# Half of the first modulation as one-column matmuls on TensorE in a hybrid decoder block

## The chip, the core and the metric

The kernel runs on one NeuronCore of a Trainium2 chip. The metric is the device time of one launch in microseconds, as the median of several runs. TensorE (PE) multiplies, VectorE (DVE) and ScalarE (ACT) work elementwise, GpSimd (POOL) works elementwise and issues a few transfers, and SyncE (SP) issues nearly all transfers.

## What is computed

```python
mod = jax.nn.silu(c) @ w_ada[l] + b_ada[l]
sh1, sc1, ga1, sh2, sc2, ga2 = jnp.split(mod[:, None, :], 6, axis=-1)
h = rmsnorm(x, ln_mix_g[l]) * (1.0 + sc1) + sh1
(rq, rk, rv, rg, nq_, nkc, nvc, ...) = jnp.split(h @ w_in[l], IN_SPLITS, axis=-1)
...
k_cmp = compress(kc, pe_k, w1_k, w2_k)
...
x = x + ga1 * (jnp.concatenate([y_ret, y_nsa], axis=-1) @ w_out[l])
h2 = rmsnorm(x, ln_ffn_g[l]) * (1.0 + sc2) + sh2
x = x + ga2 * ((jax.nn.silu(h2 @ w_ff_gate[l]) * (h2 @ w_ff_up[l])) @ w_ff_down[l])
return rmsnorm(x, ln_final_g)
```

There are 512 tokens of width 1024 and one row `c` of 1024 values. `w_ada` is 1024 x 6144; its six column blocks of 1024 give the six modulation vectors. All is float32. This case is about `sc1` (the scale half) and `sh1` (the shift half), which are needed before the first projection can start.

## The kernel before, in words

Every large product is made of three matmuls (`product`, L1085): each operand is split into a high and a low part, and high x high, high x low and low x high are added in PSUM. A unit of weights comes by one transfer of 512 KB into one of seven slots of `raw`, ACT writes its high part to `wh` (`high`, L420), and POOL writes the rest to `wl` (`low`, L370). For the activations `hTh` and `hTl` play the same parts, and they are feature-major: eight blocks `k` of 128 features by 512 tokens.

The front end of the kernel makes `hTh` and `hTl`. The tokens are normalised, PE transposes them (L1120) block by block, and ACT copies them to `xT` (L454). Then the modulation is applied in four steps `q`, each for two blocks `k = 2q` and `2q + 1`:

- **The weights.** SP loads sixteen pieces of `w_ada` of 512 KB into the eight slots of `early` (`load_early`, L313). Piece `j = 4q + 2kh + i` holds the rows of contraction half `kh` for 256 columns of step `q`; `i = 0` is the scale half, `i = 1` the shift half. A slot is loaded again when DVE has used it (`ada_used`).
- **The sums over the contraction.** `ada_early` (L682) on DVE multiplies a 128x256 part of a piece by a column of `cs` (silu of `c`) and adds it to `acc`: 16 operations for each step, 8 of the scale half and 8 of the shift half, taken in turn. They are spread over the step before by hand: the constant `AHEAD` and the ranges at L751 to L766 say how many stand before `mod_columns`, and between and behind the two `h_low`.
- **The sum over the partitions.** `modulation(q)` (L1103) on PE does it with four fp32 matmuls of one column, `acc` as the stationary operand and a column of ones as the moving one (`sum_columns`, L1097).
- **Applying it.** DVE adds the bias (`mod_columns`, L712, L716 and L720) into `mods`; ACT scales and shifts block `k` into `hf` (L462) and copies it to `hTh` (L465); DVE subtracts for `hTl` (`h_low`, L746, L748). Between two blocks ACT does the high part of the next unit of weights, whose low part POOL makes.

On PE `modulation(q + 1)` stands in the first projection chunk: the loop over units `v` at L1155 has, for `v` = 0, 1, 2, the products of tokens tile 0 and 1, then `modulation(v + 1)`, then those of tiles 2 and 3. `modulation(0)` stands among the transposes, before those of block 6. So each step is a ring: `mods` of step `q`, `hf`, `hTh`, `hTl`, the products of tiles 0 and 1 with block `2q + 1`, `modulation(q + 1)`, `mods` of step `q + 1`.

```python
                for t in range(TT):
                    if v < UPC - 1 and t == TT // 2:
                        modulation(q + 1)
```

After the fourth step DVE goes on with the other modulation vectors (`ada`, L696), whose weights share the ring `raw` with the units, so that each free slot waits for DVE or for POOL (`refill`, L295). ACT takes the first chunk out of PSUM, does the high parts of units 7 and 8, and then issues eight transfers of 256-byte rows (`load_blocks`, L501) that gather the blocks for the compression. What follows on ACT, and through it on PE, stands behind these issues.

## Time and profile before

| what | value |
|---|---|
| runs of the kernel | 825.2, 827.97, 830.14 us; median 827.97 |
| span of the profiled execution | 822.2 us |
| PE busy | 726.4 us (88%) |
| DVE busy | 323.9 us (39%) |
| ACT busy | 259.1 us (32%) |
| POOL busy | 266.8 us (32%) |

The own time of the profiled execution was not recorded beside its span; the runs lie 3.0 to 7.9 us above the span. The busy shares are means over the whole kernel: in the first 60 us, and around 93 to 147 us, PE has long stretches without work, and in most of the rest it has none.

### The profile page before, as it was taken

To read this page: it belongs to the slowest core of one execution; us is meant where nothing else is said; L and a number is where in the kernel's file an instruction comes from. 1 tells how busy PE (TensorE), PEld (TensorE's weight loads), DVE (VectorE), ACT (ScalarE), POOL (GpSimd) and SP (SyncE) were. 2 spreads that over 40 slices of the span, in tenths; PEclk is the share of its full clock that TensorE was granted. 3 is DMA by queue.
4 is the path that set the end of the run, shared out by engine and by line. 5 is a ranking of instruction groups with operands and counts; after the bars stand their busy time and mean duration, and the time that the engine had idled before them with its cause. 6 is when DMAs were issued, how large, how long until landed. Compare 5 with 4: busy or idle time off the path is not lost.

```text
span 822.2 us, 9608 instructions
## 1 busy us (share of the span) xinstructions
PE 726.4 (88%) x3715; PEld 600.0 (73%) x3715; DVE 323.9 (39%) x529; ACT 259.1 (32%) x515; POOL 266.8 (32%) x126
## 2 busy tenths in 40 slices
PE   2789400888999999999999999999999999999995
PEld 2567300678877777878888988888888888888884
DVE  4769300887653335755235301100000003943215
ACT  4433000332335335464244432222222222333222
POOL 3327000522005000211072254444444443755531
PEclk9979855899999999999999999999999999999998
DMA  9948600556633000000643052333233331332002
GB/s 317 361 171 259 233 18 18 184 186 211 215 113 103 1 2 26 1 1 2 205 119 87 2 146 86 101 103 98 86 99 102 103 103 52 128 103 94 9 1 102
DMA packets 78372, 89.39 MB, mean 109 GB/s; under 512 B 7072, under 2 KB 62072, under 8 KB 78200
## 3 DMA queue, kind: packets, MB, share of 16 engines
q1 hardware_dynamic: 73040, 86.10, 32.4%
q10 hardware_dynamic: 4872, 1.61, 0.8%
q0 software_dynamic: 416, 1.08, 0.3%
q8 instruction: 29, 0.48, 0.3%
q14 instruction: 15, 0.12, 0.1%
HBM read 86.16 MB, written 2.62 MB: 108 GB/s over the span
## 4 chain that ended last, share of the span: by engine, by line
PE 61%; DVE 1%; ACT 1%; issue 1%; POOL 0%; POOLq 0%; DVEq 0%
PE ps L1413 10%; PE ps L1414 10%; PE ps L1412 10%; PE ps L1087 8%; PE ps L1089 7%; PE ps L1088 7%; PE ps L1246 3%; PE ps L1234 2%; PE ps L1279 1%; PE ps L1269 1%; PE ps L1224 1%; ACT xb L667 0%; PE ps L1391 0%; POOL rstd L381 0%; PE ps L1289 0%
## 5 line engine op out<-in xcount | busy, mean ns | idle before, releaser
L376 POOL TENSOR_TENSOR wl<-raw,wh 128x1024 fp32r<-128x1024 f32 (+1 forms) x94 | 238.2, 2540 | 389.4 <-ACT wh L430 389.2
L430 ACT ACTIVATE wh<-raw 128x1024 fp32r<-128x1024 f32 (+1 forms) x94 | 97.1, 1037 | 192.2 <-PE ps L1414 74.0
L1087 PE MATMUL ps<-wh,hTh 128*128 128x512 f32 (+1 forms) x224 | 93.8, 419 | 65.3 <-ACT stage L483 54.2
L1412 PE MATMUL ps<-hTh,wh 128*128 128x512 f32 (+1 forms) x384 | 142.8, 372 | 0.0
L1413 PE MATMUL ps<-hTl,wh 128*128 128x512 f32 (+1 forms) x384 | 142.6, 371 | 0.0
L1414 PE MATMUL ps<-hTh,wl 128*128 128x512 f32 (+1 forms) x384 | 142.6, 371 | 0.0
L1087 PEld LDWEIGHTS ps<-wh,hTh 128*128 128x128 f32 x224 | 45.0, 201 | 76.9 <-issue 60.8
L1052 DVE TENSOR_TENSOR act<-ps,sg 128x512 f32<-128x512 f32 x22 | 15.2, 692 | 212.3 <-PE ps L1414 212.3
L1088 PE MATMUL ps<-wl,hTh 128*128 128x512 f32 (+1 forms) x224 | 88.6, 395 | 0.0
L1089 PE MATMUL ps<-wh,hTl 128*128 128x512 f32 (+1 forms) x224 | 88.5, 395 | 0.0
L1412 PEld LDWEIGHTS ps<-hTh,wh 128*128 128x128 f32 x384 | 72.3, 188 | 12.6
L1413 PEld LDWEIGHTS ps<-hTl,wh 128*128 128x128 f32 x384 | 72.3, 188 | 12.4
L1414 PEld LDWEIGHTS ps<-hTh,wl 128*128 128x128 f32 x384 | 72.3, 188 | 12.4
L1087 PE MATMUL ps<-wh,ah 128*128 128x512 f32 x176 | 68.5, 389 | 0.0
L1088 PE MATMUL ps<-wl,ah 128*128 128x512 f32 x176 | 68.5, 389 | 0.0
L1089 PE MATMUL ps<-wh,al 128*128 128x512 f32 x176 | 68.5, 389 | 0.0
L566 ACT ACTIVATE PT<-ps 128x128 f32<-128x128 f32 (+3 forms) x64 | 28.1, 439 | 89.9 <-PE ps L1234 89.7
L875 DVE TENSOR_REDUCE mn<-ps 128x1 f32<-128x128 f32 (+3 forms) x64 | 31.3, 489 | 60.3 <-PE ps L1224 57.6
L1089 PEld LDWEIGHTS ps<-wh,hTl 128*128 128x128 f32 x224 | 44.9, 200 | 8.8
L1088 PEld LDWEIGHTS ps<-wl,hTh 128*128 128x128 f32 x224 | 45.1, 201 | 6.7 <-issue 0.2
L710 DVE SCALAR_TENSOR_TENSOR acc<-raw,cs,acc 128x1024 f32<-128x1024 f32 x28 | 47.1, 1682 | 3.3 <-DMA raw<-in_w_ada 2.0
L777 DVE TENSOR_TENSOR raw<-raw,ga 128x1024 f32<-128x1024 f32 x30 | 48.2, 1632 | 0.0
(185 smaller groups left out, 975.0 us busy)
## 6 DMA issues: line engine op xcount, KB each, us to landing
raw<-in_w_ada SPq DMA_DIRECT2D x32, 512.0 KB, 5.6
raw<-in_w_ff_gate SPq DMA_DIRECT2D x22, 512.0 KB, 3.8
raw<-in_w_ff_up SPq DMA_DIRECT2D x22, 512.0 KB, 3.7
raw<-in_w_ff_down SPq DMA_DIRECT2D x22, 512.0 KB, 3.3
raw<-in_w_in SPq DMA_DIRECT2D x20, 512.0 KB, 5.7
early<-in_w_ada SPq DMA_DIRECT2D x16, 512.0 KB, 9.7
raw<-in_w_out SPq DMA_DIRECT2D x8, 512.0 KB, 3.3
xs<-in_x SPq DMA_DIRECT2D x4, 512.0 KB, 6.0
```

The source lines that it names most:

```text
L376: pool.tensor_tensor(lo, raw[:, slot, 0:n], hi.bitcast(F32), ALU.subtract).then_inc(w_lo, 1)
L430: a.activation(split(u, n)[0], raw[:, slot, 0:n], ACT.Copy).then_inc(w_hi, 1)
L566: a.activation(PT[:, n % 2, 0:w], ps[:, 2, 0:w], ACT.Copy).then_inc(pT_ok, 1)
L710: d.scalar_tensor_tensor(dst, raw[:, slot, :], cs[:, k:k + 1], dst, ALU.mult, ALU.add).then_inc(ada_used, 1)
L777: d.tensor_tensor(raw[:, slot, :], raw[:, slot, :], ga[:, :], ALU.mult).then_inc(w_scaled, 1)
L875: d.tensor_reduce(mn[:, n % 8:n % 8 + 1], ps[:, s_bank(n), 0:w], AX.X, ALU.min).then_inc(s_min, 1)
L1087: mm(o, ah_, bh_, start=first, stop=False)
L1088: mm(o, ah_, bl_, start=False, stop=False)
L1089: return mm(o, al_, bh_, start=False, stop=last)
L1412: mm(o, hi[:, ks], hTh[:, k, c0:c1], start=k == 0, stop=False)
L1413: mm(o, hi[:, ks], hTl[:, k, c0:c1], start=False, stop=False)
L1414: ins = mm(o, lo[:, ks], hTh[:, k, c0:c1], start=False, stop=k == KT - 1)
```

## The change

In each step the shift half no longer goes through `acc`. PE takes the loaded pieces of `early` as the stationary operand, 128x128 at a time, and a column of `cs` as the moving one, and adds the eight parts of the contraction in PSUM: 16 one-column fp32 matmuls in each step. The scale half stays on DVE, 8 operations in each step in place of 16, and PE sums it with two of the four former matmuls. The slots of the shift half are now free when PE has done its matmuls (`shift_sum`), and `AHEAD` and the ranges are halved.

```diff
-AHEAD = 4
+AHEAD = 2
-ADA_OPS = 4 * ADA_START
+ADA_OPS = 2 * ADA_START
...
-        return 8 * (j // 2 + 1) - (j + 1) % 2 if j < ADA_START else ADA_OPS + j - ADA_START + 1
+        return 4 * (j // 2 + 1) if j < ADA_START else ADA_OPS + j - ADA_START + 1
...
-                if j >= EARLY:
+                q, kh, i = j // 4, j // 2 % 2, j % 2
+                if j >= EARLY and i == 0:
                     sp.wait_ge(ada_used, ada_ops(j - EARLY))
-                q, kh, i = j // 4, j // 2 % 2, j % 2
+                elif j >= EARLY:
+                    sp.wait_ge(shift_sum, q - 1)
...
-                for o in ops:
-                    p, (kk, i) = 2 * q + o // 8, divmod(o % 8, 2)
-                    j, k = 2 * p + i, 4 * (p % 2) + kk
+                for k in ops:
+                    kh, kk = divmod(k, 4)
+                    j = 4 * q + 2 * kh
...
-                    dst = acc[:, i, 2 * q * P:2 * (q + 1) * P]
+                    dst = acc[:, 0, 2 * q * P:2 * (q + 1) * P]
...
-                        d.wait_ge(ada_used, 16 * q + o - 1)
+                        d.wait_ge(ada_used, 8 * q + k)
...
-            ada_early(0, range(16))
+            ada_early(0, range(KT))
...
-                    ada_early(q + 1, range(AHEAD, AHEAD + 3))
+                    ada_early(q + 1, range(AHEAD, AHEAD + 2))
                 h_low(2 * q)
                 if q < UPC - 1:
-                    ada_early(q + 1, range(AHEAD + 3, AHEAD + 5))
+                    ada_early(q + 1, range(AHEAD + 2, AHEAD + 3))
                 h_low(2 * q + 1)
                 if q < UPC - 1:
-                    ada_early(q + 1, range(AHEAD + 5, 16))
+                    ada_early(q + 1, range(AHEAD + 3, KT))
...
-                pe.wait_ge(ada_used, 16 * (q + 1))
                 if q:
                     pe.wait_ge(mod_read, q)
-                sum_columns(0, 4 * q, (2 * q, 2 * q + 1))
-                sum_columns(1, 4 * q + 2, (2 * q, 2 * q + 1)).then_inc(mod_sum, 1)
+                else:
+                    pe.wait_ge(c_silu, 1)
+                for b in range(2):
+                    for k in range(KT):
+                        kh, kk = divmod(k, 4)
+                        j = 4 * q + 2 * kh + 1
+                        if b == 0 and kk == 0:
+                            pe.wait_ge(early_in[j % EARLY], 16 * (j // EARLY + 1))
+                        c0 = (2 * kk + b) * P
+                        ins = mm(ps[:, 7, 4 * q + 2 + b:4 * q + 3 + b], early[:, j % EARLY, c0:c0 + P], cs[:, k:k + 1],
+                                 start=k == 0, stop=k == KT - 1)
+                ins.then_inc(shift_sum, 1)
+                pe.wait_ge(ada_used, 8 * (q + 1))
+                sum_columns(0, 4 * q, (2 * q, 2 * q + 1)).then_inc(mod_sum, 1)
```

The order on PE around `modulation(0)`: L1120 are the transposes, L1100 the one-column matmuls of `modulation`, and the 128x512 rows are the products of unit 0. Before:

```order
L1120 MATMUL ps<-cst,xs 128x128 x24
L1100 MATMUL ps<-ones,acc 128x1 x4
L1120 MATMUL ps<-cst,xs 128x128 x8
L1087 MATMUL ps<-wh,hTh 128x512
L1088 MATMUL ps<-wl,hTh 128x512
```

And in the changed kernel, where the lines have moved down by 3 to 14:

```order
L1134 MATMUL ps<-cst,xs 128x128 x24
L1119 MATMUL ps<-cs,early 128x1 x16
L1103 MATMUL ps<-ones,acc 128x1 x2
L1134 MATMUL ps<-cst,xs 128x128 x8
L1090 MATMUL ps<-wh,hTh 128x512
L1091 MATMUL ps<-wl,hTh 128x512
```

The four one-column matmuls have become eighteen at the same place; at the three later places, behind 12, 36 and 60 matmuls of the projection, the same happens. The order on DVE in the first step (L716 and L720 make `mods`, L748 is `h_low`), before:

```order
L691 TENSOR_SCALAR acc<-early,cs 128x256 x2
L694 SCALAR_TENSOR_TENSOR acc<-early,cs,acc 128x256 x2
L716 TENSOR_TENSOR mods<-ps,cols 128x2
L720 TENSOR_TENSOR mods<-mods,cols 128x2
L716 TENSOR_TENSOR mods<-ps,cols 128x2
L694 SCALAR_TENSOR_TENSOR acc<-early,cs,acc 128x256 x3
L748 TENSOR_TENSOR hTl<-hf,hTh 128x512
L694 SCALAR_TENSOR_TENSOR acc<-early,cs,acc 128x256 x2
L748 TENSOR_TENSOR hTl<-hf,hTh 128x512
L694 SCALAR_TENSOR_TENSOR acc<-early,cs,acc 128x256 x7
```

And in the changed kernel:

```order
L694 TENSOR_SCALAR acc<-early,cs 128x256
L697 SCALAR_TENSOR_TENSOR acc<-early,cs,acc 128x256
L719 TENSOR_TENSOR mods<-ps,cols 128x2
L723 TENSOR_TENSOR mods<-mods,cols 128x2
L719 TENSOR_TENSOR mods<-ps,cols 128x2
L697 SCALAR_TENSOR_TENSOR acc<-early,cs,acc 128x256 x2
L751 TENSOR_TENSOR hTl<-hf,hTh 128x512
L697 SCALAR_TENSOR_TENSOR acc<-early,cs,acc 128x256
L751 TENSOR_TENSOR hTl<-hf,hTh 128x512
L697 SCALAR_TENSOR_TENSOR acc<-early,cs,acc 128x256 x3
```

The places stay, and the counts go from 4, 3, 2, 7 to 2, 2, 1, 3. On SP the order of the transfers stays, and the third group of pieces now waits for two engines in turn (in the kernel before, all four wait for `ada_used`):

```order
L308 DMA raw<-in_w_in 128x2x512
L322 DMA early<-in_w_ada 128x4x256 [waits ada_used]
L322 DMA early<-in_w_ada 128x4x256 [waits shift_sum]
L322 DMA early<-in_w_ada 128x4x256 [waits ada_used]
L322 DMA early<-in_w_ada 128x4x256 [waits shift_sum]
L335 DMA cst<-in_consts 128x902
L308 DMA raw<-in_w_in 128x2x512
```

Behind the waiting pieces stand, in the queue, the constants, the units of weights 2 and 3, and the first loads of `ada`.

## Rows read from the trace of the kernel before

**Rows 1.** The page: span and part 1 (busy us, share, instructions).

```profile
span 822.2 us, 9608 instructions
PE 726.4 (88%) x3715; PEld 600.0 (73%) x3715; DVE 323.9 (39%) x529; ACT 259.1 (32%) x515; POOL 266.8 (32%) x126
```

**Rows 2.** Waits, 0 to 70 us: us in total, times, longest.

```profile
ACT hf L462 <- DVE mods L716: 21.9, 3, 8.2
DVE mods L716 <- PE ps L1100: 3.6, 3, 1.7
```

**Rows 3.** Timeline of ACT: start, us, instruction, idle before it and releaser.

```profile
24.90 0.60 ACT L454 ACTIVATE xT<-ps 128x512 f32<-128x512 f32 x1 [0.25 <-PE ps L1120]
25.40 0.80 ACT L462 ACTIVATE hf<-xT,mods 128x512 f32<-128x512 f32 x1
...
36.45 0.82 ACT L462 ACTIVATE hf<-xT,mods 128x512 f32<-128x512 f32 x1 [7.28 <-DVE mods L716]
...
48.46 0.81 ACT L462 ACTIVATE hf<-xT,mods 128x512 f32<-128x512 f32 x1 [8.21 <-DVE mods L716]
...
58.63 0.82 ACT L462 ACTIVATE hf<-xT,mods 128x512 f32<-128x512 f32 x1 [6.38 <-DVE mods L716]
```

**Rows 4.** Timeline of PE: the four modulations and what stands ahead of them.

```profile
21.35 1.71 PE L1100 MATMUL ps<-ones,acc 128*128 128x1 f32 x8
...
31.20 0.79 PE L1087 MATMUL ps<-wh,hTh 128*128 128x512 f32 x1 [1.85 <-DVE hTl L748]
...
35.01 0.94 PE L1100 MATMUL ps<-ones,acc 128*128 128x1 f32 x8
...
42.26 0.79 PE L1087 MATMUL ps<-wh,hTh 128*128 128x512 f32 x1 [2.53 <-DVE hTl L748]
...
46.26 1.70 PE L1100 MATMUL ps<-ones,acc 128*128 128x1 f32 x8
...
54.30 0.49 PE L1087 MATMUL ps<-wh,hTh 128*128 128x512 f32 x1 [0.93 <-DVE hTl L748]
...
57.08 1.05 PE L1100 MATMUL ps<-ones,acc 128*128 128x1 f32 x8 [0.42 <-DVE acc L694]
```

**Rows 5.** Timeline of DVE: early sums, `h_low`, and the first operation of `ada`.

```profile
15.38 5.62 DVE L694 SCALAR_TENSOR_TENSOR acc<-early,cs,acc 128x256 f32<-128x256 f32 x14
...
40.28 1.92 DVE L748 TENSOR_TENSOR hTl<-hf,hTh 128x512 fp32r<-128x512 f32 x1 [0.84 <-ACT hTh L465]
42.13 2.85 DVE L694 SCALAR_TENSOR_TENSOR acc<-early,cs,acc 128x256 f32<-128x256 f32 x7
...
61.51 0.69 DVE L748 TENSOR_TENSOR hTl<-hf,hTh 128x512 fp32r<-128x512 f32 x1 [0.68 <-ACT hTh L465]
62.12 0.75 DVE L707 TENSOR_SCALAR acc<-raw,cs 128x1024 f32<-128x1024 f32 x1
```

**Rows 6.** Windows: us, busy time by engine, granted clock, DMA share, GB/s.

```profile
41.00:42.00 1.00, 0.00 (x0) 0.00 (x0) 1.00 (x1) 0.00 (x0) 1.00 (x2) 0.79 1.04 408
42.00:51.00 9.00, 8.74 (x25) 7.20 (x26) 6.90 (x21) 2.51 (x4) 1.40 (x1) 0.50 0.76 292
51.00:52.00 1.00, 1.00 (x4) 0.81 (x3) 0.45 (x2) 0.97 (x2) 0.97 (x1) 0.59 0.00 0
```

**Rows 7.** Timeline of PE: long series of small fp32 matmuls, later in the kernel.

```profile
192.72 7.25 PE L1191 MATMUL ps<-flatT,w 128*128 128x64 f32 x64
...
223.11 1.84 PE L1100 MATMUL ps<-ones,acc 128*128 128x1 f32 x16
```

**Rows 8.** Timeline of ACT from 78 to 144 us: `load_blocks`.

```profile
77.96 1.06 ACT L430 ACTIVATE wh<-raw 128x1024 fp32r<-128x1024 f32 x1 [4.88 <-DMA raw<-in_w_in]
...
78.80 22.50 ACTq L512 DMA_DIRECT2D flat<-kv_scratch  x1
101.33 6.97 ACTq L511 DMA_DIRECT2D flat<-kv_scratch  x1
```

**Rows 9.** Timeline of SP: pieces 12 to 15 of `early`.

```profile
27.20 7.28 SPq L319 DMA_DIRECT2D early<-in_w_ada  x4
```

More of the change, by code:

```diff
@@ L251, in block_kernel @@
         y_ps, y_scaled = sem("y_ps"), sem("y_scaled")
+        shift_sum = sem("shift_sum")
         dve_step = sem("dve_step")
```

## The prediction

> **What bounds the kernel now.** I read the page first. PE is busy for 88% of the span and DVE for 39% [rows 1], which says nothing yet about a change that moves work from DVE to PE: what counts is who is waited for in the first 60 us. So I read the waits of 0 to 70 us. The largest on ACT is for `mods`, 21.9 us in three waits, and DVE itself makes `mods` only after waiting for the one-column matmuls L1100 on PE [rows 2]. Then I followed the ring of one step through the timelines of ACT, DVE and PE. The first blocks of the four steps start on ACT at 25.40, 36.45, 48.46 and 58.63 us [rows 3]. In the step that begins at 36.45, the second `h_low` ends at 40.28 + 1.92 = 42.20 us and releases PE at 42.26; PE does nine matmuls of 512 columns until 46.26, then the modulation for 1.70 us, and ACT starts the next step at 48.46 [rows 3 to 5]. DVE had finished its seven sums at 42.13 + 2.85 = 44.98 us, 1.3 us before PE came to the modulation [rows 4, 5]. So in this ring PE is on the path and the early sums of DVE are not. Only in the last step does PE wait for DVE, for 0.42 us [rows 4]. For `modulation(0)` both are level: the fourteen sums and what precedes them end at 15.38 + 5.62 = 21.0, the transposes at 21.35 [rows 4, 5].
>
> The end of this ring is passed on in full. The first `ada` operation starts on DVE as the last `h_low` ends, at 62.1 us [rows 5]. The slot of unit 8 comes free through that chain of `ada` operations, ACT waits 4.88 us for unit 8, and right behind it stand the gather transfers, whose issuing holds ACT for 66 us, eight of them at 7 us or more each [rows 8]. Nothing in that stretch can catch up a late start.
>
> **TensorE's clock.** One modulation of four matmuls (eight records) takes 1.70 to 1.71 us at 21.35 and 46.26, and 0.94 to 1.05 us at 35.01 and 57.08 [rows 4]. The window of 42 to 51 us shows a granted clock of 0.50, which is the 1.2 GHz level [rows 6]; the row at 21.35 costs the same, so PE is slow there too (the record shows 1.00 up to 41 us, where it has no event yet). The nine matmuls ahead of a modulation take 35.01 - 31.20 = 3.81 and 46.26 - 42.26 = 4.00 us, slow, and 57.08 - 0.42 - 54.30 = 2.36 us, fast. So one fp32 matmul of one column costs 1.71 / 4 = 0.43 us slow and 0.94 / 4 = 0.235 us fast. In a longer fast series eight of them take 1.84 us, 0.23 each, and 32 fp32 matmuls of 64 columns take 7.25 us, also 0.23 each [rows 7]: the price is that of loading the stationary operand, and does not fall with the number of columns.
>
> **The change, part by part.**
>
> *Removed:* two of the four `sum_columns` matmuls and eight sums on DVE in each step. A sum costs 5.62 / 14 = 0.40 us [rows 5], so DVE gets back 8 x 0.40 = 3.2 us in each step, 12.8 in all. Only the 0.42 us for which PE waited counts; the rest lay beside PE. The new wait in each sum, for the sum just before it rather than for the last but one, may make each up to 0.1 us dearer; eight of them are still shorter than sixteen were. If PE were no longer in front, this cover would be gone, but it gets longer.
>
> *Added:* sixteen one-column matmuls in each step. No row shows one with `early` as the stationary operand, but L1100 has the same form, fp32, 128x128 against 128x1. I take its price. Eighteen then cost 18 x 0.43 = 7.7 us slow or 18 x 0.235 = 4.2 us fast. They stand in PE's queue ahead of `mods`, and behind them ACT's `hf`, DVE's `h_low` and PE's own products.
>
> *Step 0.* The shift pieces 1 and 3 have long landed, as DVE already sums from pieces 0 to 3 from 15.38 us without a wait. PE is slow at 21.35: 7.7 - 1.7 = **+6.0** (fast: +2.5). The transposes of blocks 6 and 7 are behind it, and ACT must copy block 7 before the first `hf`, as it does at 24.90 [rows 3], so the whole is passed on.
>
> *Step 1.* Before, nine matmuls slow (3.81) and then a fast modulation of 0.94. The clock rose just ahead of it. In the changed kernel PE comes out of 7.7 us of small matmuls and transposes, which had not raised the clock at 21.35 either, has a gap as before, and does only nine dense matmuls. I take slow: 7.7 - 0.9 = **+6.8** (fast: 4.2 - 0.9 = +3.3).
>
> *Step 2.* Before, all slow: 4.00 + 1.70 = 5.70. Behind the long modulation PE has fifteen slow products (6.4 us at 0.43) with hardly a gap before the second `h_low` comes, 5.8 us after `mods` (36.4 to 42.2); such a run raised the clock before. I take the nine fast (2.4) and, as the columns leave the array nearly empty, a clock that falls within them: three quarters fast, 18 x 0.284 = 5.1. That is 7.5 - 5.7 = **+1.8** (all fast: 6.6 - 5.7 = +0.9; all slow: 3.9 + 7.7 - 5.7 = +5.9).
>
> *Step 3.* Before, fast: 2.36 + 0.42 + 1.05 = 3.83. Now 7.5: **+3.7** (all fast: 6.6 - 3.8 = +2.8; all slow: 11.6 - 3.8 = +7.8).
>
> *Transfers.* Piece 9 now waits for PE's sixteen of step 0, to about 21.35 + 16 x 0.43 = 28 us, and piece 13 for those of step 1, to about 48 us; the four pieces 12 to 15 had been issued from 27.20 to 34.5 us before [rows 9]. Queued behind piece 13 are two more pieces, unit 3, unit 4, unit 5 and three `ada` loads: with it nine loads of 0.5 MB, 4.7 MB, which at the 408 GB/s of [rows 6] take 12 us, to 60. The first of them to be needed is unit 3, by ACT early in step 2 at about 65 us by the sum above. I cost it at nothing; if that cover were gone, it would be a few us more.
>
> **The sum:** 6.0 + 6.8 + 1.8 + 3.7 = +18.3 us. Against the profiled span it is 822.2 + 18.3 = 840.5; the runs lie 3 to 8 us above the span, the median 5.8, so 828.0 + 18.3 = **846 us**. The bounds are 2.5 + 3.3 + 0.9 + 2.8 = +9.5 (fast throughout, 837.5) and 6.0 + 6.8 + 5.9 + 7.8 = +26.5 (slow throughout, 854.5).
>
> **The rivals.**
>
> *A. The columns are nearly free (not slower).* One mechanism: the stationary operand is loaded beside the matmul before, and a matmul of one column then costs next to nothing. The modulations would shrink from 1.7 + 0.9 + 1.7 + 1.05 = 5.4 us to at most half, and the 0.42 us go: -3.1, 825 us. It decides from the point where a column costs under 4 / 18 of 0.235 us, 0.05 us. Against it stand all rows: 64 columns cost as much as one, 0.23 us [rows 7]. The Trainium skill (TensorE: Matmul & The Clock Gate, Back-to-back issue gap) gives about 25 ns for matmuls of 1 to 64 columns, and by that alone eighteen, each in two records, would be an estimated 0.9 us; the rows contradict it for this form. Chance 3%.
>
> *B. Slow throughout.* The small matmuls let the clock fall at once, and it has not risen again when the nine products come: 854.5 us. For it speaks that the clock stayed at 0.50 from 42 to 51 us although PE was busy for 8.74 of 9.00 us, with one modulation among it [rows 6]. Chance 20%.
>
> *C. Fast throughout.* The clock fell at 41 us after a gap ahead of 42.26 [rows 4, 6]. If the small matmuls count as work, they close the gaps and PE stays fast: 837.5 us, or 841 if only step 0 is slow. The same page (Why this matters for your kernels) asks for TensorE to be kept busy without gaps, which speaks for this. Against it: 10 us of transposes and columns had not raised the clock by 28 us, as the nine slow matmuls from 31.20 show. Chance 20%.
>
> *D. The queue of SP.* Units or pieces behind the wait for `shift_sum` come late: some 3 to 8 us more, 849 to 854. Chance 6%.
>
> *E. Less collision.* The second gather transfer takes 22.5 us to issue and a later one 7.0 [rows 8], because weight loads run beside it. If the gather came later against those loads, up to 15.5 us would return: 846 - 15.5 = 830.5, no change. But ACT and the loads both hang on the same DVE chain and shift together. Chance 2%.
>
> **How the numbers follow.** The forecast has 49%, B 20, C 20, D 6, A 3, E 2. The range of 838 to 855 holds the forecast, B, D and most of C. A measurement can tell 0.5%, 4 us, from no change: slower 0.95 (the forecast, B, C, D), same 0.04 (E and most of A), faster 0.01.
>
> **What would show it.** L1119 should take some 0.21 us a record slow and 0.115 fast, 32 records in each step. The first `hf` of the steps should start near 31.4, 49, 63 and 77 us in place of [rows 3]; DVE should end its sums earlier against PE, and PE should wait for none of them. The first `ada` operation and the gather should be 18 us later, and all behind them the same as before. I am wrong if records of L1119 take under 0.06 us, if `hf` of step 0 starts before 28 us, or if the distance from the last `h_low` to the gather changes by over 2 us.

## The result, and the profile after

| what | before | after |
|---|---|---|
| runs | 825.2, 827.97, 830.14 us | 843.06, 843.09, 843.45 us |
| median | 827.97 us | 843.09 us |
| ratio after / before | | 1.0204 [1.0168, 1.0241] |
| span of the profiled execution | 822.2 us | 841.3 us |
| time of the profiled execution | not recorded | 843.06 us |

The change makes the kernel slower by 2.0%, 16.9 us by the ratio; the two medians alone differ by 15.1 us. The time lies inside the predicted range of 838 to 855 us and 2.9 us under the 846 of the forecast. (An execution now and then takes some 50 us longer, with a mean granted clock near 0.88, whatever the kernel; these are left out of every median and ratio, and the one profile that fell into one, that of the eighth experiment below, is read only up to 60 us.)

Wherever both are on record, the time of an execution is some 1.8 us above its span. The profiled execution before, with its span of 822.2 us, therefore took an estimated 824.0 us, less than any of the three runs, and the difference of the two spans, 19.1 us, is larger than that of the runs.

The page of the changed kernel, the lines that answer to [rows 1]:

```profile
span 841.3 us, 9773 instructions
PE 749.3 (89%) x3827; PEld 623.1 (74%) x3827; DVE 312.7 (37%) x497; ACT 258.8 (31%) x515; POOL 263.7 (31%) x126
```

PE has 112 records more (64 matmuls more, in two records each, less the 16 records of the eight matmuls that are gone) and is busy for 22.9 us longer. DVE has 32 operations less and is busy for 11.2 us less. The waits of the changed kernel, 0 to 90 us, in the columns of [rows 2]:

```profile
ACT hf L465 <- DVE mods L719: 33.5, 3, 13.9
DVE mods L719 <- PE ps L1103: 24.7, 4, 9.3
```

ACT now waits 33.5 us for `mods`, where it was 21.9, and DVE waits 24.7 us for the one-column matmuls on PE, where it was 3.6. DVE is early and PE is late: the same ring, bound more firmly by the same engine. The one-column matmuls by tile, shortest, median and longest in ns, first and last start (records overlap, so the price of one is the length of a series by its count, not a record's own length):

```profile
L1119 PEld LDWEIGHTS ps<-cs,early x128: 187/200/338, 19.8 to 71.1; 128*128 128x128 f32 x128
L1119 PE MATMUL ps<-cs,early x128: 164/250/353, 19.9 to 71.2; 128*128 128x1 f32 x128
```

and the four modulations in the timeline of PE, which answer to [rows 4]:

```profile
13.71 4.30 PE L1134 MATMUL ps<-cst,xs 128*128 128x128 f32 x16 [4.23 <-DVE xs L739]
18.91 1.14 PE L1134 MATMUL ps<-cst,xs 128*128 128x128 f32 x8 [0.90 <-ACT xT L457]
19.89 4.99 PE L1119 MATMUL ps<-cs,early 128*128 128x1 f32 x32
24.74 0.99 PE L1103 MATMUL ps<-ones,acc 128*128 128x1 f32 x4
25.59 1.95 PE L1134 MATMUL ps<-cst,xs 128*128 128x128 f32 x8
...
33.59 0.80 PE L1090 MATMUL ps<-wh,hTh 128*128 128x512 f32 x1 [1.56 <-DVE hTl L751]
...
37.59 6.82 PE L1119 MATMUL ps<-cs,early 128*128 128x1 f32 x32
44.27 0.99 PE L1103 MATMUL ps<-ones,acc 128*128 128x1 f32 x4
...
51.33 0.50 PE L1090 MATMUL ps<-wh,hTh 128*128 128x512 f32 x1 [0.62 <-DVE hTl L751]
...
53.50 4.50 PE L1119 MATMUL ps<-cs,early 128*128 128x1 f32 x32
57.87 0.99 PE L1103 MATMUL ps<-ones,acc 128*128 128x1 f32 x4
...
64.93 0.51 PE L1090 MATMUL ps<-wh,hTh 128*128 128x512 f32 x1 [0.58 <-DVE hTl L751]
...
67.11 4.46 PE L1119 MATMUL ps<-cs,early 128*128 128x1 f32 x32
71.43 0.99 PE L1103 MATMUL ps<-ones,acc 128*128 128x1 f32 x4
```

No idle time stands before any of the L1119 or L1103 groups: PE comes straight out of products (or transposes), does sixteen columns on `early`, and finds the sums of DVE done long before. A step slow throughout shows 6.82 / 32 = 0.213 us a record; the three others (4.99, 4.50, 4.46) lie between that and the fast price, because the clock fell inside them. The windows of step 0 show the fall itself (columns as in [rows 6]):

```profile
18.90:21.90 3.00, 2.99 (x27) 2.93 (x27) 1.41 (x2) 2.40 (x5) 1.98 (x1) 1.00 1.08 348
22.00:25.60 3.60, 3.60 (x19) 3.60 (x19) 0.00 (x0) 0.00 (x0) 0.00 (x0) 0.50 1.08 363
```

PE is busy without a gap in both, and the granted clock goes from the 2.4 GHz level to that of 1.2 GHz at 21.95 us. The steps on ACT, and the gather, which answer to [rows 3] and [rows 8]:

```profile
28.07 0.80 ACT L465 ACTIVATE hf<-xT,mods 128x512 f32<-128x512 f32 x1
...
45.77 0.82 ACT L465 ACTIVATE hf<-xT,mods 128x512 f32<-128x512 f32 x1 [13.91 <-DVE mods L719]
...
59.36 0.81 ACT L465 ACTIVATE hf<-xT,mods 128x512 f32<-128x512 f32 x1 [9.80 <-DVE mods L719]
...
72.92 0.81 ACT L465 ACTIVATE hf<-xT,mods 128x512 f32<-128x512 f32 x1 [9.77 <-DVE mods L719]
...
92.06 1.06 ACT L433 ACTIVATE wh<-raw 128x1024 fp32r<-128x1024 f32 x1 [4.84 <-DMA raw<-in_w_in]
92.90 23.93 ACTq L515 DMA_DIRECT2D flat<-kv_scratch  x1
```

The first blocks of the steps are late by 2.7, 9.3, 10.9 and 14.3 us: the four steps cost 2.7, 6.7, 1.6 and 3.4 us. The first `ada` operation on DVE answers to [rows 5]:

```profile
14.61 4.02 DVE L697 SCALAR_TENSOR_TENSOR acc<-early,cs,acc 128x256 f32<-128x256 f32 x7
...
76.40 0.75 DVE L710 TENSOR_SCALAR acc<-raw,cs 128x1024 f32<-128x1024 f32 x1
```

It is 14.3 us late (62.12 before). The whole span in the two profiles, as a chain of four stretches:

| stretch | before | after | difference |
|---|---|---|---|
| to the first `ada` operation | 62.1 | 76.4 | +14.3 |
| from there to the end of the last gather issue | 81.7 | 82.7 | +1.0 |
| from there to the first transpose of `mix` on PE | 129.6 | 133.4 | +3.8 |
| from there to the end | 548.8 | 548.8 | 0 |

(With the rounding of the ends, that is the 19.1 us between the two spans.) The second and the third line are not the change's; the section on the stretch behind the gather comes to them.

### The profile page after: what moved, and what is told of

Same layout as the page of the kernel before. It is cut to its first block, busy times and chain, and to the rows that moved or that the text cites. A ratio compares the mean times of both kernels' runs of the same rounds, so it can differ in the third digit from the quotient of the medians.

```text
span 841.3 us, 9773 instructions
## 1 busy us (share of the span) xinstructions
PE 749.3 (89%) x3827; PEld 623.1 (74%) x3827; DVE 312.7 (37%) x497; ACT 258.8 (31%) x515; POOL 263.7 (31%) x126
## 4 chain that ended last, share of the span: by engine, by line
PE 60%; DVE 1%; ACT 1%; issue 1%; POOL 0%; POOLq 0%; DVEq 0%
PE ps L1428 10%; PE ps L1427 10%; PE ps L1426 10%; PE ps L1090 8%; PE ps L1092 7%; PE ps L1091 7%; PE ps L1260 3%; PE ps L1248 2%; PE ps L1293 1%; PE ps L1283 1%; PE ps L1238 1%; ACT xb L670 0%; PE ps L1405 0%; POOL rstd L384 0%; PE ps L1303 0%
## 5 line engine op out<-in xcount | busy, mean ns | idle before, releaser
L379 POOL TENSOR_TENSOR wl<-raw,wh 128x1024 fp32r<-128x1024 f32 (+1 forms) x94 | 235.1, 2507 | 411.3 <-ACT wh L433 411.2
L1090 PE MATMUL ps<-wh,hTh 128*128 128x512 f32 (+1 forms) x224 | 95.6, 427 | 61.9 <-ACT stage L486 54.8
L1090 PEld LDWEIGHTS ps<-wh,hTh 128*128 128x128 f32 x224 | 46.7, 208 | 72.6 <-issue 59.4
L1092 PE MATMUL ps<-wh,hTl 128*128 128x512 f32 (+1 forms) x224 | 90.6, 404 | 0.0
L1091 PE MATMUL ps<-wl,hTh 128*128 128x512 f32 (+1 forms) x224 | 90.3, 403 | 0.0
L1428 PEld LDWEIGHTS ps<-hTh,wl 128*128 128x128 f32 x384 | 72.4, 188 | 12.3
L569 ACT ACTIVATE PT<-ps 128x128 f32<-128x128 f32 (+3 forms) x64 | 28.1, 438 | 91.8 <-PE ps L1248 91.6
L713 DVE SCALAR_TENSOR_TENSOR acc<-raw,cs,acc 128x1024 f32<-128x1024 f32 x28 | 45.1, 1610 | 4.9 <-DMA raw<-in_w_ada 3.7
```

What stands on the lines that cost most here:

```text
L379: pool.tensor_tensor(lo, raw[:, slot, 0:n], hi.bitcast(F32), ALU.subtract).then_inc(w_lo, 1)
L569: a.activation(PT[:, n % 2, 0:w], ps[:, 2, 0:w], ACT.Copy).then_inc(pT_ok, 1)
L713: d.scalar_tensor_tensor(dst, raw[:, slot, :], cs[:, k:k + 1], dst, ALU.mult, ALU.add).then_inc(ada_used, 1)
L1090: mm(o, ah_, bh_, start=first, stop=False)
L1091: mm(o, ah_, bl_, start=False, stop=False)
L1092: return mm(o, al_, bh_, start=False, stop=last)
```

## The experiments

All ratios are to runs of the kernel before on the same chip at the same time. "Front" below is the shift of the first `ada` operation against the 62.12 us of [rows 5], in one profile of each kernel.

| kernel | median us | ratio [95%] | first `hf` of the steps | front | gather end to `mix` |
|---|---|---|---|---|---|
| before | 825 to 828 | | 25.4, 36.5, 48.5, 58.6 | | 129.6 |
| after | 843.09 | 1.0204 [1.0168, 1.0241] | 28.1, 45.8, 59.4, 72.9 | +14.3 | 133.4 |
| 1 columns only | 841.70 | 1.0196 [1.0161, 1.0231] | 31.1, 46.0, 60.4, 75.5 | +16.9 | 131.8 |
| 2 no columns | 824.32 | 0.9992 [0.9956, 1.0028] | 23.1, 35.3, 46.0, 55.2 | -3.4 | 132.0 |
| 3 sum sooner | 828.60 | 1.0031 [0.9993, 1.0070] | 25.1, 36.1, 46.3, 57.3 | -1.4 | 135.3 |
| 4 sums ahead | 824.36 | 0.9994 [0.9952, 1.0037] | 24.6, 35.5, 45.7, 56.6 | -2.0 | 129.6 |
| 5 half dose | 833.48 | 1.0062 [1.0033, 1.0092] | 26.0, 38.2, 50.2, 61.7 | +3.0 | 135.4 |
| 6 filler | 825.57 | 0.9968 [0.9938, 0.9997] | 24.3, 34.8, 45.0, 55.2 | -3.5 | 137.2 |
| 7 columns in the gap | 836.85 | 1.0108 [1.0073, 1.0143] | 31.0, 44.2, 56.1, 68.0 | +9.4 | 131.9 |
| after again | 840.27 | one run | 31.1, 45.7, 58.1, 71.7 | +13.0 | 131.9 |
| 8 filler and sums ahead | 826.13 | 0.9989 [0.9962, 1.0016] | 23.8, 34.7, 44.9, 55.1 | -3.6 | not read |
| 9 after with filler | 842.65, 841.36 | 1.0186 [1.0131, 1.0241] | 30.7, 43.0, 56.5, 70.6 | +11.9 | 135.3 |

### 1. The columns alone, without the relief of DVE

The kernel before, with fourteen one-column matmuls more in each modulation: eighteen on PE as in the changed kernel, all of DVE's sums kept.

```diff
                 sum_columns(0, 4 * q, (2 * q, 2 * q + 1))
+                for _ in range(7):
+                    sum_columns(1, 4 * q + 2, (2 * q, 2 * q + 1))
                 sum_columns(1, 4 * q + 2, (2 * q, 2 * q + 1)).then_inc(mod_sum, 1)
```

> The kernel before with only PE's part of the change: fourteen more one-column fp32 matmuls in each modulation (the two of the shift half are issued eight times), so eighteen as in the changed kernel; DVE's sums and SP's waits stay as before. Theory (the path goes through PE's eighteen columns): as slow as the changed kernel, 843 us, up to 846 since PE may again wait for DVE; the first blocks of steps 1 to 3 start on ACT about 9, 11 and 14 us later than before. Rival (the cost is in SP's wait for shift_sum or in the serial chain of sums on DVE): no slower than before, 828 us, and the columns hidden.

Measured: 1.0196 [1.0161, 1.0231], the ratio of the changed kernel within its interval. The timeline of PE of this kernel, steps 0 to 2:

```profile
21.08 7.68 PE L1100 MATMUL ps<-ones,acc 128*128 128x1 f32 x36
...
40.65 4.84 PE L1100 MATMUL ps<-ones,acc 128*128 128x1 f32 x36
...
54.60 5.31 PE L1100 MATMUL ps<-ones,acc 128*128 128x1 f32 x36 [0.44 <-DVE acc L694]
```

36 records take 7.68 us slow, 0.213 each, whether the stationary operand is `acc` or `early`. What follows: the cost of the change is the cost of these matmuls at this place on PE. The operations taken off DVE, the chained sums and the new wait of SP are in the changed kernel and not in this one, and the two ratios agree. The intervals leave room for some 3 us between them, and the front of this profile is 2.6 us later than that of the changed kernel: PE waits here for DVE's last sum for 0.44 us in each of the steps 2 and 3, and step 0 was slow throughout, which in the changed kernel's first profile it was not. The fourth first block came 16.9 us late, where 14 had been expected.

### 2. The relief of DVE alone

The changed kernel with the sixteen columns left out, the waits for `early` and the release of its slots kept (the shift half of the modulation is not computed).

```diff
-                for b in range(2):
-                    for k in range(KT):
...
-                        ins = mm(ps[:, 7, 4 * q + 2 + b:4 * q + 3 + b], early[:, j % EARLY, c0:c0 + P], cs[:, k:k + 1],
-                                 start=k == 0, stop=k == KT - 1)
-                ins.then_inc(shift_sum, 1)
+                for kh in range(2):
+                    j = 4 * q + 2 * kh + 1
+                    pe.wait_ge(early_in[j % EARLY], 16 * (j // EARLY + 1))
                 pe.wait_ge(ada_used, 8 * (q + 1))
+                sum_columns(0, 4 * q + 2, (2 * q, 2 * q + 1)).then_inc(shift_sum, 1)
                 sum_columns(0, 4 * q, (2 * q, 2 * q + 1)).then_inc(mod_sum, 1)
```

> The changed kernel without its sixteen columns in each step: DVE's eight sums, AHEAD and SP's two kinds of waits stay as changed; the shift half is left out (its two columns are summed from the scale half by two matmuls, so there are four as before). Theory: the cost is gone, 827 to 829 us, and what DVE gives back is worth at most 0.5 us. Rival (SP's waits, late loads or the serial chain on DVE cost part of it): 832 to 843 us. Second rival (DVE's relief is worth several us that the columns hid): 822 to 825 us.

Measured: 0.9992 [0.9956, 1.0028], no change. In its profile ACT begins the fourth step 3.4 us earlier than before:

```profile
55.20 0.82 ACT L465 ACTIVATE hf<-xT,mods 128x512 f32<-128x512 f32 x1 [5.39 <-DVE mods L719]
```

but that does not show in the time. Of the 3.4 us, 2.3 are in step 0, where the transposes began 1.0 us earlier, and the last of them ahead of the modulation and the modulation itself ran fast (1.14 and 1.12 us, where they took 1.97 and 1.71 before); the steps 1 to 3 are shorter by 1.1 us together. What follows: with the columns gone, the whole cost of the change is gone, and what halving DVE's sums is worth lies between a gain of 3.6 and a loss of 2.3 us, the ends of the interval. Runs 1 and 2 together settle the cause.

### 3 and 4. Where the modulation stands

If PE's place in the ring is what counts, the kernel before might gain by an earlier `modulation`. Run 3 puts it behind the products of tile 0 in place of tile 1 (two products, that is six matmuls, less ahead of it); DVE's sums are then the later ones. Run 4 does this and moves three more of the sums ahead of the second `h_low`.

```diff
-                    if v < UPC - 1 and t == TT // 2:
+                    if v < UPC - 1 and t == 1:
                         modulation(q + 1)
```

> The kernel before with modulation(q + 1) placed behind the products of token tile 0 instead of tile 1, six matmuls sooner in each of three steps; nothing else. Theory (the ring of a step goes through what stands on PE ahead of the modulation): steps 1 and 2 shorter by 1.0 to 1.5 us each, until DVE's last sum is the bound (it ended 1.3 us before PE came), step 3 by nothing: 825 to 827 us. Rival (the ring is bound elsewhere): 828 to 829 us.

```diff
-                    ada_early(q + 1, range(AHEAD + 3, AHEAD + 5))
+                    ada_early(q + 1, range(AHEAD + 3, AHEAD + 8))
                 h_low(2 * q + 1)
                 if q < UPC - 1:
-                    ada_early(q + 1, range(AHEAD + 5, 16))
+                    ada_early(q + 1, range(AHEAD + 8, 16))
```

> As e3_sum_sooner, and three more of DVE's sums ahead of the second h_low of a step, where DVE waits for ACT and POOL for 2.3 us. Theory: DVE's last sum comes 1.2 us sooner, PE is the bound again with three matmuls ahead of the modulation: each of three steps 1.3 to 2.6 us shorter than before, 821 to 825 us. Rival (h_low is held up by the sums): no faster than e3_sum_sooner.

Measured: 1.0031 [0.9993, 1.0070] and 0.9994 [0.9952, 1.0037]. In the profiles the front is 1.4 and 2.0 us earlier, and neither is faster by its runs. What was expected of the steps came true in neither. The steps 1 to 3 took 10.9, 10.2 and 11.0 us in run 3 and 10.9, 10.2 and 10.9 us in run 4, where they took 11.05, 12.01 and 10.17 before: only step 2 got shorter, step 3 got longer, and run 4 was to shorten each of them by 1.3 to 2.6 us. In run 3 PE now waits 1.13, 1.19 and 1.81 us for DVE's last sum, so that six matmuls less on PE are replaced by a wait. A gain of 1 or 2 us is below what four runs can tell; that it exists in the front is read from one profile each.

### 5. Half the dose

Run 1 with six matmuls more in each step in place of fourteen.

```diff
+                for _ in range(3):
+                    sum_columns(1, 4 * q + 2, (2 * q, 2 * q + 1))
```

> As e1_pe_only with six more columns in each modulation instead of fourteen (ten in all). Theory (each column on PE is passed on in full at 0.235 to 0.43 us): 24 more columns in all, so 6 / 14 of the 16.7 us of e1_pe_only, plus 5 to 10 us against the kernel before. Rival (a few columns hide in PE's gaps, and only many reach the path): under 3 us.

Measured: 1.0062 [1.0033, 1.0092], which is +5.1 us for 24 matmuls, 0.21 us each (+6.8 us, 0.28 each, by the medians of 833.48 and 826.64); run 1 had +16.2 us (1.0196 of 825) for 56, 0.29 us each. The +5.1 us are at the lower end of the 5 to 10 us expected. The timeline of PE:

```profile
20.17 3.50 PE L1100 MATMUL ps<-ones,acc 128*128 128x1 f32 x20 [0.28 <-DVE acc L694]
...
35.40 2.29 PE L1100 MATMUL ps<-ones,acc 128*128 128x1 f32 x20
```

Step 1 is fast here (2.29 / 20 = 0.115 us a record). The price of run 1 lies between the fast 0.23 and the slow 0.43 us; that of the shorter series is near the fast one, with an interval of 0.11 to 0.32. The intervals (2.7 to 7.6 us against 13.3 to 19.1) keep the two doses apart; they don't show that the cost grows faster than the count.

### 6. A clock held up

The kernel before with matmuls that nothing reads: six of 512 columns before the first product, five behind the first product of tile 0 in the steps 1 to 3, where PE otherwise waits for `hTl`.

```diff
+            pe.wait_ge(w_hi, 1)
+            for _ in range(6):
+                mm(ps[:, 6, :], wh[:, 0, 0:P], wh[:, 0, 0:512], start=True, stop=True)
...
+                        if v < UPC - 1 and t == 0 and kk == 0:
+                            for _ in range(5):
+                                mm(ps[:, 6, :], hTh[:, 0, 0:P], hTh[:, 0, :], start=True, stop=True)
```

> The kernel before, with matmuls of 512 columns into an unused PSUM bank put where PE waits in the ring: six behind the last transposes, five behind the first three products of each of the units 0 to 2. Nothing reads them. Theory (part of the ring's time is the slow clock that follows PE's gaps): the clock does not fall between 38 and 52 us, the nine products and the modulation of step 2 take 2.4 + 0.9 us in place of 4.0 + 1.7, and the last first block starts on ACT 2 to 4 us sooner; the whole is 0 to 4 us faster, as far as later stretches do not take it back. Rival (the fillers stand in the way and the clock comes by chance): first blocks at the same time or later, 825 to 830 us.

The timeline of PE, the modulations of the steps 1 to 3:

```profile
33.13 1.05 PE L1100 MATMUL ps<-ones,acc 128*128 128x1 f32 x8 [0.41 <-DVE acc L694]
...
43.38 1.05 PE L1100 MATMUL ps<-ones,acc 128*128 128x1 f32 x8 [0.44 <-DVE acc L694]
...
53.62 1.05 PE L1100 MATMUL ps<-ones,acc 128*128 128x1 f32 x8 [0.44 <-DVE acc L694]
```

All three are fast, the steps take 10.51, 10.24 and 10.16 us where they took 11.05, 12.01 and 10.17, and the front is 3.5 us earlier. At most 2.3 us of this are the filler's: the first block of step 0 was already 1.1 us earlier on ACT, behind a modulation that ran fast before the first filler stood on PE (22.59 us). Now PE waits for DVE in every step: with a fast clock the ring is level between the two. Measured: 0.9968 [0.9938, 0.9997], some 2.6 us, just outside no change. It is one of nine ratios, and run 8, which has the same filler, doesn't repeat it, so the gain is not certain. The Trainium skill (TensorE: Matmul & The Clock Gate, Why this matters for your kernels) advises to keep TensorE busy without gaps; this profile agrees, with a granted clock of 1.00 from 26 us to the end of the ring, where before it fell at 41.6 us in a gap of 2.53 us [rows 4, 6]. What that is worth is the 0.3% of the ratio, if anything.

### 7. The columns in PE's gap

The changed kernel with its columns for step 1 to 3 behind the first product of tile 0, where PE used to wait for the second `h_low`, and the rest of the modulation before tile 1.

```diff
-            def modulation(q):
+            def shift_columns(q):
...
+            def modulation(q):
+                if q == 0:
+                    shift_columns(0)
                 pe.wait_ge(ada_used, 8 * (q + 1))
...
-                    if v < UPC - 1 and t == TT // 2:
+                    if v < UPC - 1 and t == 1:
                         modulation(q + 1)
...
+                        if v < UPC - 1 and t == 0 and kk == 0:
+                            shift_columns(q + 1)
```

> The changed kernel with the sixteen columns of step q + 1 put where PE waits for the second h_low (behind the first three products of a unit), and the two sums of the scale half behind tile 0 instead of tile 1. Theory (PE is nearly full in the changed ring: 24 products and 18 columns in 13.6 us with gaps of 0.6 us): only the gaps can be filled, 1 to 3 us faster than the changed kernel, 840 to 843 us, and far from the kernel before. Rival (what costs is only the place of the columns ahead of the modulation): near the kernel before, 828 to 832 us.

Measured: 1.0108 [1.0073, 1.0143], 836.85 us, about 8 us better than the changed kernel, and 3 us better than the edge of what was expected. The timeline of PE:

```profile
34.75 6.82 PE L1119 MATMUL ps<-cs,early 128*128 128x1 f32 x32
...
49.92 3.63 PE L1119 MATMUL ps<-cs,early 128*128 128x1 f32 x32
```

The columns are fast in the later steps (3.63 / 32 = 0.113 us a record), and yet the steps take 13.2, 11.9 and 11.95 us. The rival, that hidden columns cost nothing, is not reached: no idle time stands before these rows either, so PE has no gap left and still adds the columns to every step. PE's gap in the kernel before was 0.93 to 2.53 us a step [rows 4], and no gap of that size hides sixteen columns at 3.6 us.

### The changed kernel once more

> The changed kernel unaltered, for a second profile. Theory: the slow and fast stretches of PE lie otherwise, so each of the four steps moves by up to some 2 us and the stretch from the gather to the end by up to some 4 us, while the order of the waits stays; first blocks on ACT within 3 us of the first profile, one time of 840 to 846 us. Rival (the ring repeats exactly): all within 0.5 us.

A second profile of the changed kernel, the same code. Its timeline of PE:

```profile
19.31 1.97 PE L1134 MATMUL ps<-cst,xs 128*128 128x128 f32 x8 [0.91 <-ACT xT L457]
21.07 6.82 PE L1119 MATMUL ps<-cs,early 128*128 128x1 f32 x32
...
40.62 3.81 PE L1119 MATMUL ps<-cs,early 128*128 128x1 f32 x32
...
53.48 3.62 PE L1119 MATMUL ps<-cs,early 128*128 128x1 f32 x32
...
65.78 4.53 PE L1119 MATMUL ps<-cs,early 128*128 128x1 f32 x32
```

and of ACT:

```profile
31.09 0.80 ACT L465 ACTIVATE hf<-xT,mods 128x512 f32<-128x512 f32 x1
```

Here step 0 is slow and costs 31.09 - 25.40 = 5.7 us, and step 1, slow in the first profile (6.82), is fast (3.81): 3.5 us in place of 6.7. The two profiles of one kernel differ by 3 us in a single step, more than the 2 us expected, and by 1.3 us at the end of the front. In windows of 1 us the granted clock falls from 1.00 to 0.50 three times between 20 and 77 us in each: at 21.95, 56.0 and 69.7 us in the first profile, each time inside a series of columns, and at 44.4, 58.0 and 68.3 us in the second, of which only the last is inside the columns on `early` and the other two come up to 1.1 us behind their end. **Where the clock falls differs from execution to execution; how often it falls in the ring was the same in both.**

### 8. Filler and sums ahead, for a version that beats both

Run 6 together with run 4, to get rid of the wait for DVE that run 6 brought out.

> e6_filler and e4_sums_ahead together. In e6_filler PE is fast through the whole ring and waits 0.41 to 0.44 us for DVE's last sum ahead of each of the three later modulations, so the order of the sums is on the path there. Theory: each of three steps 1.3 to 2 us shorter than in e6_filler (10.2 to 10.5 us), the first ada operation near 54 us in place of 58.7, and the whole 3 to 5 us faster than e6_filler, 821 to 823 us where the kernel before has 826. Rival (ACT and POOL bound the step once PE is fast): steps as in e6_filler, 825 us.

Measured: 0.9989 [0.9962, 1.0016], no better than run 6. The steps 1 to 3 take 10.9, 10.2 and 10.1 us and the first `ada` operation comes at 58.54 us: the rival, not the theory. The second `h_low` now stands behind five sums on DVE, which take 4.18 us together. The tile `acc` in that stretch (25.9 to 30.2 us; columns as above), in ns:

```profile
L694 DVE SCALAR_TENSOR_TENSOR acc<-early,cs,acc x5: 472/480/2597, 25.9 to 29.6; 128x256 f32<-128x256 f32 x5
```

the timeline of POOL:

```profile
26.89 2.55 POOL L376 TENSOR_TENSOR wl<-raw,wh 128x1024 fp32r<-128x1024 f32 x1 [4.38 <-ACT wh L430]
```

and that of DVE:

```profile
25.94 4.18 DVE L694 SCALAR_TENSOR_TENSOR acc<-early,cs,acc 128x256 f32<-128x256 f32 x5
30.04 0.68 DVE L748 TENSOR_TENSOR hTl<-hf,hTh 128x512 fp32r<-128x512 f32 x1
```

and of PE, which waits for it:

```profile
30.78 0.50 PE L1087 MATMUL ps<-wh,hTh 128*128 128x512 f32 x1 [2.53 <-DVE hTl L748]
```

Four of the sums are as long as ever (0.48 us) and one lasts 2.6 us, as long as the operation that POOL does in that time. In run 6 it is `h_low` itself that is held up there: it takes 1.66 us in place of 0.68 and ends at 30.31 us, 0.4 us earlier than here. The sums spared behind `h_low` were paid ahead of it, and in both kernels it is POOL's operation that `h_low` comes behind (more on this in the last section). No version that was run beats the kernel before by more than the 0.3% of run 6.

### 9. The changed kernel with the filler of run 6

If the cost of the columns is mostly a slow clock, holding the clock up should give a part of it back.

> The changed kernel with the fillers of e6_filler. Theory (about a third of the changed kernel's cost is slow clock, and the columns themselves let the clock fall): the nine products of each step are fast, the columns partly; steps 1 to 3 of 11.5 to 13.5 us in place of 17.7, 13.6, 13.6, 836 to 841 us. Rival (the columns alone keep PE slow and the fillers only add to it): 843 to 850 us. If the whole cost were the clock: near 830 us.

Measured: 1.0186 [1.0131, 1.0241], of two runs. The timeline of PE:

```profile
20.72 6.82 PE L1119 MATMUL ps<-cs,early 128*128 128x1 f32 x32
...
38.46 3.63 PE L1119 MATMUL ps<-cs,early 128*128 128x1 f32 x32
...
50.80 4.36 PE L1119 MATMUL ps<-cs,early 128*128 128x1 f32 x32
...
64.66 4.54 PE L1119 MATMUL ps<-cs,early 128*128 128x1 f32 x32
```

Only step 1 is fast to its end. The granted clock falls again at 43.3, 53.5 and 67.1 us, the first time 1.2 us behind the columns on `early`, the other times inside them, although PE has no gap there. The steps 1 to 3 take 12.3, 13.5 and 14.1 us, the last one outside the 11.5 to 13.5 expected. The front comes back by 2.4 and 1.1 us against the first and the second profile of the changed kernel; expected was 836 to 841 us, and the two runs gave 841.36 and 842.65, no gain that can be told from the changed kernel. In this kernel the clock falls at the columns without a gap on PE.

### The stretch behind the gather

The windows view from the end of the gather to the first transpose of `mix`; the numbers are the width, the busy times of PE, PEld, DVE, ACT and POOL, the granted clock, the DMA share and GB/s. Before:

```profile
143.80:273.40 129.60, 120.38 (x684) 99.72 (x685) 83.36 (x151) 47.04 (x134) 34.98 (x17) 0.95 0.49 161
```

After:

```profile
159.10:292.50 133.40, 123.94 (x684) 102.72 (x685) 83.19 (x151) 46.95 (x134) 35.52 (x17) 0.91 0.48 156
```

Run 6, where the gather ended 2.1 us earlier than before:

```profile
141.70:278.90 137.20, 127.77 (x683) 105.10 (x684) 83.36 (x151) 47.02 (x134) 34.92 (x17) 0.89 0.47 152
```

The same 684 records of matmuls (one is missing in some) take 129.6 to 137.2 us, and the stretch gets longer as the mean granted clock goes from 0.95 to 0.89. In eleven profiles it is 129.6 at 0.95 (before, run 4), about 132 at 0.92 or 0.93 (runs 1, 2, 7, the changed kernel again), 133.4 at 0.91 (after), and 135.3 to 137.2 at 0.89 (runs 3, 5, 6, 9). It doesn't follow the edits: run 4 with an early gather has the shortest, run 6 with an early gather the longest, and the two profiles of the changed kernel have 133.4 and 131.9.

The stretch ahead of it, from the first `ada` operation to the end of the last gather issue, was 81.7 us before and 82.2 to 83.5 us in the ten other profiles, so the +1.0 us of the table of stretches is not the change's either. What stands behind, from the first transpose of `mix` to the end, is 548.8 us in all eleven. So these profiles differ in the first 290 us or so and nowhere else, and the profile of the kernel before happened to be the shortest in one of the two middle stretches and level with the shortest in the other.

It fits the spread of the runs of one kernel (the kernel before took 822 to 833 us in all runs shown here). Of 27 runs of it on one chip, the four with a mean granted clock of 0.933 took 830.95 to 831.49 us and the five with 0.954 or more 823.91 to 827.92 us, though the longest, 833.38 us, had 0.949. A spread of this size is enough to hide a front that is 1.4 to 3.6 us earlier, as in the runs 2, 3, 4 and 8. That the clock in this stretch varies by itself, from where its falls happen to lie, is what the table suggests; it was not tested by profiling one kernel many times.

## Why the prediction was right, point by point

**What bounds the kernel: right.** PE was on the ring and DVE's sums were not. Taking eight sums off each step gave nothing measurable (run 2), adding the matmuls alone gave the whole cost (run 1). One link of the ring is missing in the prediction, without harm to the sum: the 1.92 us of the second `h_low` are three times its usual 0.69, and it ends only when POOL has made the low part of the unit (last section). Its account of the gather is off in a detail too: the first of the eight transfers took 0.74 us to issue, the second 22.50, and only the others about 7.

**The price of a column: right.** 0.43 us slow and 0.235 fast were forecast for `early` as the stationary operand from rows that had `acc`. Measured: 6.82 / 16 = 0.43 and 3.63 / 16 = 0.23.

**Step 0 (+6.0 forecast): wrong in the first profile, right in the second.** +2.7 and +5.7 us. The step that failed is "PE is slow at 21.35", carried over to the changed kernel. In the first profile the transposes at 18.91 already ran fast (1.14 us for what takes 1.97), only transposes stood before them on PE from 13.71, and the columns began 1.5 us earlier (19.89 against 21.35), 0.7 of it because the transposes themselves began earlier. The modulation then took 25.59 - 19.89 = 5.7 us, 3.6 of it after the fall at 21.95. With `hf` at 28.07 us the profile just missed one of the prediction's own signs of being wrong, a start before 28. With that the sentence against rival C, that transposes and columns "had not raised the clock", falls: in the profile before they had not, in this one they had.

**Steps 1 to 3 (+6.8, +1.8, +3.7): right.** Measured +6.7, +1.6, +3.4. Step 1 came out slow as taken; in the second profile it was fast, +3.5, so that this agreement is partly the luck of one execution, as the two profiles traded step 0 against step 1. For step 2 and 3 the reasoning of fast products (53.50 - 51.33 = 2.2 us) and a fall within the columns is what the rows show: 4.50 and 4.46 us lie between the fast 3.6 and the slow 6.8. (In the second profile the columns of step 2 were fast to their end, 3.62 us, and the step cost only 0.4 us more than before.) The two matmuls of L1103 behind them then came slow (0.99).

**DVE: the direction right, a size off.** "Up to 0.1 us dearer" for a chained sum was too little: 4.02 / 7 = 0.57 against 0.40, 0.17 dearer. It stayed hidden, as eight are still shorter than sixteen.

**SP and rival D: nothing there.** Unit 3 was issued at 45.96 us and used by ACT at 60.74 without a wait, and run 1, which has none of SP's new waits, takes the same time.

**Behind the ring: passed on in full.** "All behind them the same as before" holds for the chain from the last `h_low` to the gather (15.9 us before, 15.7 after) and for the last 548.8 us. The issuing of the gather took 67.0 us in place of 65.8, so that rival E's return isn't seen. The stretch up to `mix` took 3.8 us more, for which the prediction had no term.

**The sum.** The front gave 14.3 of the 18.3 forecast; 1.0 and 3.8 us from behind it filled the span up to +19.1. Measured over the runs it is +16.9 [13.9, 20.0] by the ratio, against +18.3. The sum was so near the spans partly by luck: step 0 was forecast too high, and the stretches behind the front, in which the profile before was a short one, were missing.

**The rivals.** A (columns nearly free) is refuted by the record itself: 0.113 us at the least on average over 32. B, slow throughout, isn't seen: in each of the two profiles at least one step has fast columns or products. C, fast throughout (837.5 or 841), has in its 841 the number nearest to the 843.09 us of the runs; by the ratio its +13.0 is farther from +16.9 than the forecast's +18.3. The second profile, slow in step 0 and fast in most of steps 1 to 3, is close to it at 840.27. But its mechanism, that the columns count as work and hold the clock, is not what is seen: the clock falls inside the columns or up to 1.2 us behind their end, without a gap on PE, at all nine falls in the two profiles and in run 9.

## What to carry to other kernels

Before moving work to the engine with less pressure, find out which engine the ring of that stage waits for; here DVE at 39% and PE at 88% pointed the right way, but the waits of the first 60 us said it exactly. An fp32 matmul of a 128x128 stationary operand with one column took 0.23 us at the fast clock, as much as one with 64 columns [rows 7], while the loads of the stationary operands kept PE's loader busy without a break (3.60 of 3.60 us in the window from 22.00). So a product with one column pays for the whole stationary operand, and it should stay off PE where PE is on the ring. The form with the large operand moving was not tried. And if a profile of one execution shows a gain under one per cent in one stage, compare the same stretches of later stages first: with TensorE's clock moving, identical instructions differed by 7.6 us of 130.

## What was not expected of the hardware

- **fp32 transposes can bring the clock up.** After 16 of them from 13.71 us, with no other work on PE but two matmuls before 10 us, the next eight took 1.14 us in the changed kernel's first profile and 1.97 in its second. Of all twelve profiles they were fast in five (after, runs 2, 5, 6 and 8) and slow in seven. The Trainium skill (TensorE: Matmul & The Clock Gate, Part 4: PE-mode transpose) says that the full clock isn't engaged for transposes; these five profiles differ from that, and there the measurement decides.
- **A busy PE with one-column matmuls lets it fall.** From 18.90 to 21.90 us PE was busy for 2.99 us of 3.00, and the granted clock fell at 21.95; from 22.00 to 25.60 us it was busy for 3.60 us of 3.60 and had 0.50. The same happened in or behind three series in run 9, filler or not. So a share of busy time near 100% was no sign of a fast clock in this ring.
- **Some of DVE's operations last until POOL's is done.** `h_low` takes 0.69 us with POOL idle, and 1.65 to 1.97 us when it starts while POOL makes a low part [rows 5]. In step 1 of the kernel before it ran from 40.28 to 42.20 us; the timeline of POOL has

```profile
39.02 2.63 POOL L376 TENSOR_TENSOR wl<-raw,wh 128x1024 fp32r<-128x1024 f32 x1 [8.43 <-ACT wh L430]
```

which ends at 41.65, 0.55 us earlier. All 18 long `h_low` of six profiles (before, both of the changed kernel, runs 1, 6 and 7) end 0.54 to 0.56 us behind the end of POOL's operation. So in each of the first three steps this operation of POOL's is a link of the ring, between ACT's high part and PE's products. It holds sums as well: one of five took 2.6 us beside a POOL operation of 2.55 us (run 8). Another time POOL was the one that took longer, 4.27 us from 19.21 us in the kernel before, while DVE's series of sums went on. Why one holds the other, and what a shorter operation on POOL would give, no run was made for. Apart from that, a sum takes 0.40 us where two chains alternate (5.62 / 14) and 0.57 in one chain (4.02 / 7).
